# Modulation and first seven projections by slices of 256 features, and the second norm's scale rows moved to the output projection

## The reference

```python
mod = silu(c) @ w_ada + b_ada                      # six vectors of 1024
shift1, scale1, gate1, shift2, scale2, gate2 = split(mod, 6)
h = rms_norm(x, norm1_g) * (1 + scale1) + shift1
q, k, v, qi, ki, wi, u, g_attn, g_pool = split_cols(h @ w_in, IN_SIZES)
# index scores relu(qi ki) wi choose 128 keys for each query; attention; pooling over u
merged = sigmoid(g_attn) * y_attn + sigmoid(g_pool) * y_pool
x = x + gate1 * (merged @ w_out)
h2 = rms_norm(x, norm2_g) * (1 + scale2) + shift2
x = x + gate2 * conv_ffn(h2)
```

## Time and profile before

| | us |
|---|---|
| Median of 3 runs | 754.72 |
| Lowest and highest | 754.32, 757.94 |
| The profiled execution | 759.15 |
| Its span | 757.2 |
| TensorE busy in it | 739.7 (98%) |
| VectorE, ScalarE, GpSimd busy | 379.0, 306.6, 312.3 |

### The profile page before, as it was taken

One profiled execution on the slowest core, in us unless ns is written; L12 is line 12 of the kernel. 1 busy time (PEld: TensorE's weight loads), 2 busy tenths in 40 slices (PEclk: granted clock), 3 DMA queues, 4 the chain that ended last, 5 costly groups with the idle time before them and its releaser, 6 DMA issues.

```text
span 757.2 us, 9497 instructions
## 1 busy us (share of the span) xinstructions
PE 739.7 (98%) x3568; PEld 597.2 (79%) x3568; DVE 379.0 (50%) x693; ACT 306.6 (40%) x501; POOL 312.3 (41%) x165
## 2 busy tenths in 40 slices
PE   4989999999999999999999999999999999999997
PEld 3467788888777777887899888888788888888886
DVE  2588699972446551774685435464443433004002
ACT  4224513256756763334455343434334343212120
POOL 1125338562623332547423444444444444443431
PEclk9969989999999999999999999999999999999999
DMA  8995511221113113644338344323323321233301
GB/s 327 381 338 204 187 55 57 71 97 56 57 57 112 57 56 107 262 159 128 97 95 267 112 111 112 91 76 112 101 68 110 111 99 68 84 112 112 137 2 56
DMA packets 83995, 92.75 MB, mean 122 GB/s; under 512 B 2035, under 2 KB 66287, under 8 KB 83951
## 3 DMA queue, kind: packets, MB, share of 16 engines
q1 hardware_dynamic: 82719, 87.43, 35.6%
q10 hardware_dynamic: 1232, 4.72, 1.7%
HBM read 90.05 MB, written 2.10 MB: 122 GB/s over the span
## 4 chain that ended last, share of the span: by engine, by line
PE 96%; DVE 1%; DMA 1%; ACT 1%; SPq 0%; issue 0%; DVEq 0%; ACTq 0%
PE bank L1471 42%; PE bank L1491 21%; PE bank L1480 21%; PE bank L1547 2%; PE bank L1741 1%; PE bank L1719 1%; PE bank L1707 1%; PE bank L1513 1%; PE bank L1625 1%; DMA xtok<-in_x_dram 1%; PE bank L1565 1%; PE bank L1614 1%; ACT junk L747 1%; PE bank L1518 1%; PE bank L1775 1%; PE bank L1532 0%
## 5 line engine op out<-in xcount | busy, mean ns | idle before, releaser
L650 POOL TENSOR_TENSOR wsplit<-stage,wsplit 128x1024 fp32r<-128x1024 f32 (+1 forms) x120 | 275.0, 2295 | 395.2 <-ACT wsplit L732 391.7
L1471 PE MATMUL bank<-hT,wsplit 128*128 128x512 f32 (+1 forms) x1264 | 295.3, 386 | 0.0
L1471 PEld LDWEIGHTS bank<-hT,wsplit 128*128 128x128 f32 x1264 | 231.8, 190 | 46.5 <-issue 0.9
L732 ACT ACTIVATE wsplit<-stage 128x1024 fp32r<-128x1024 f32 (+1 forms) x120 | 119.8, 1000 | 280.9 <-PE bank L1480 196.7
L1480 PE MATMUL bank<-hT,wsplit 128*128 128x512 f32 (+1 forms) x632 | 152.8, 384 | 0.0
L1480 PEld LDWEIGHTS bank<-hT,wsplit 128*128 128x128 f32 x632 | 114.7, 188 | 23.5 <-issue 0.8
L1491 PE MATMUL bank<-wsplit,guT 128*128 128x512 f32 x528 | 119.8, 389 | 0.0
L1491 PEld LDWEIGHTS bank<-wsplit,guT 128*128 128x128 f32 x528 | 99.1, 188 | 20.5
L1429 DVE SCALAR_TENSOR_TENSOR yb<-bank,conv,yb 128x511 f32<-128x511 f32 (+1 forms) x44 | 32.9, 749 | 65.1 <-ACT yb L1022 64.3
L1429 DVE SCALAR_TENSOR_TENSOR ya<-bank,conv,ya 128x511 f32<-128x511 f32 (+1 forms) x44 | 33.0, 749 | 59.2 <-ACT ya L1022 58.4
L1364 DVE TENSOR_TENSOR tmp_last<-bank,gate_row 128x512 f32<-128x512 f32 x8 | 5.5, 688 | 101.7 <-PE bank L1491 101.7
(11 more groups left out here) (188 smaller groups left out, 731.8 us busy)
## 6 DMA issues: line engine op xcount, KB each, us to landing
stage<-in_w_up_dram SPq DMA_DIRECT2D x44, 512.0 KB, 5.2
stage<-in_w_in_dram SPq DMA_DIRECT2D x17, 1024.0 KB, 5.3
stage<-in_w_down_dram SPq DMA_DIRECT2D x10, 1024.0 KB, 5.0
ada_early<-in_w_ada_dram SPq DMA_DIRECT2D x8, 1024.0 KB, 10.1
ada<-in_w_ada_dram SPq DMA_DIRECT2D x7, 1024.0 KB, 11.7
ada_mid<-in_w_ada_dram ACTq DMA_DIRECT2D x4, 1024.0 KB, 8.1
stage<-in_w_out_dram SPq DMA_DIRECT2D x4, 1024.0 KB, 6.1
ada_last<-in_w_ada_dram SPq DMA_DIRECT2D x4, 1024.0 KB, 11.1
```

The costliest lines, as they stand in the source:

```text
L650: pool.tensor_tensor(unit_split(n, 1), unit_source(n), unit_split(n, 0).bitcast(F32), ALU.subtract).then_inc(low, 1)
L732: me.did(act.activation(unit_split(n, 0), unit_source(n), ACT.Copy), high)
L1471: pe.matmul(out_bank[:, tokens], hi[:, k, :], rhs[:, part, k, tokens], start=k == 0 and part == 0, stop=False)
```

## The change

The start is worked by four slices of 256 features. SP loads for slice q all 1024 rows of the 256 columns of vectors 0 and 1 (2 MB in four transfers of 1 KB pieces) and then one stage item that holds, for two feature blocks, the weights of all seven first units (896 columns). The small vectors are loaded by ScalarE's queue. x is scaled by the inverse root token by token on VectorE before it is turned, into all eight banks. TensorE adds up a slice of the two vectors with a padded c as weights, four groups of 32 output rows in one bank; ScalarE copies the bank, four one-column products add the rows up. VectorE and ScalarE make two blocks of `hT`, and VectorE, no longer GpSimd, makes the low parts of the first eight weight units. TensorE then runs the seven units together for each block.

The index dots, sums and relus stand within v0 and v1; v comes before u. The rows of vector 3 (shift2) are added up during the first products, from eight loads of 512 KB; those of vector 4 (scale2) go by `ada_mid` and stand on VectorE ahead of `gate_vector(0)`, its column sums on TensorE behind the first tile of the second half.

```diff
-ROW_TURN = {1: 0, 3: 1, 4: 2, 2: 3, 5: 4}
+ROW_TURN = {3: 0, 2: 1, 4: 2, 5: 3}
+FIRST = (("qi", 0), ("qi", 1), ("kw", 0), ("q", 0), ("q", 1), ("q", 2), ("q", 3))
+KS = 896
+KQ = KD // 2
...
+            def load_first(q):
+                for half in range(2):
+                    ks = slice(half * KQ, (half + 1) * KQ)
+                    for j in range(2):
+                        c0 = j * D + 2 * q * P
+                        sp.dma_start(ada_first[q][:, ks, 2 * j * P:2 * (j + 1) * P], ada[:, ks, c0:c0 + 2 * P]
+                                     ).then_inc(ada_in[q][half], 16)
...
+            def load_row(k):
+                if k % 4 == 0:
+                    sp.wait_ge(sums_ok, k // 4 + 1)
+                sp.dma_start(ada_row[k][:, :], ada[:, k, 3 * D:4 * D]).then_inc(ada_row_in[k], 16)
             for n, item in enumerate(sch.items):
-                if n == NSTAGE:
-                    for q in range(KD // 2):
-                        load_early(3, q)
+                if n < KQ:
+                    load_first(n)
...
                 load_item(n)
+                if n == KQ - 1:
+                    for k in range(KD):
+                        load_row(k)
...
# ScalarE
             for t in range(NT):
+                act.wait_ge(x_in[t], 16)
                 me.did(act.activation(junk[:, t % 2, :], xtok[:, t, :], ACT.Square,
                                       accum_out=tstat[:, 0, t:t + 1]), x_sum)
+                me.settle()
+                me.did(act.activation(tstat[:, 2, t:t + 1], tstat[:, 0, t:t + 1], ACT.Sqrt, bias=eps[:, 0:1],
+                                      scale=1.0 / D), root_ok)
+            act.wait_ge(x_t, NT)
+            for k in range(0, KD, 2):
+                me.did(act.activation(xT[:, k, :], banks[k][:, :], ACT.Copy), x_kept[0])
+            for q in range(KQ):
+                act.wait_ge(sums_ok, q + 1)
+                me.did(act.activation(rowsum[:, :], OB[:, :], ACT.Copy), row_ok)
+                high_parts(2 * q + 1)
+                for k in (2 * q, 2 * q + 1):
+                    act.wait_ge(n_ok, k + 1)
+                    me.did(act.activation(hT[:, 0, k, :], full1[:, k % 2, :], ACT.Copy), h_hi)
+                high_parts(2 * q + 2)
...
             def load_mid(n):
...
+                j, q = (2, 4)[n // 4], n % 4
+                act.dma_start(ada_mid[n % 2][:, :, :], ada[:, 2 * q:2 * q + 2, j * D:(j + 1) * D]
                               ).then_inc(ada_mid_in[n % 2], 16)
...
+            load_mid(4)
+            load_mid(5)
             high_parts(sch.unit["out", 1, NT - 1] + 1)
+            load_mid(6)
+            load_mid(7)
# VectorE
+            for q in range(KQ):
+                first_vectors(q)
+                for k in (2 * q, 2 * q + 1):
...
+                    me.did(dve.tensor_scalar(full1[:, k % 2, :], xT[:, k, :], gs[:, 0, k:k + 1], mod[:, k:k + 1],
+                                             ALU.mult, ALU.add), n_ok)
+                for k in (2 * q, 2 * q + 1):
+                    first_low(k)
+                    low_parts(k + 1)
+                for k in ((), (0, 1, 2), (3, 4, 5, 6), (7,))[q]:
+                    mod_row_of(3, k)
...
             merged_low(KD - 1)
+            for q in range(KD // 2):
+                mod_rows(4, q)
             gate_vector(0)
# TensorE
+            def first_sums(q):
+                if q == 0:
+                    pe.wait_ge(c_pad, 1)
+                    pe.wait_ge(x_kept[1], 1)
+                else:
+                    pe.wait_ge(first_mod, q)
+                for half in range(2):
+                    pe.wait_ge(ada_in[q][half], 32)
+                    for g in range(KQ):
+                        k = half * KQ + g
+                        mm = pe.matmul(OB[32 * g:32 * (g + 1), :], cpad[:, k, :], ada_first[q][:, k, :],
+                                       start=half == 0, stop=half == 1)
+                mm.then_inc(sums_ok, 1)
...
+            first_sums(0)
+            first_columns(0)
...
+            for k in range(KD - 1):
+                first_products(k, h_hi, 0, 0, start=k == 0)
+                if k % 2:
+                    first_columns(k // 2 + 1)
+                first_products(k, h_lo, 1, 0)
+                first_products(k, h_hi, 0, 1).then_inc(used, 1)
+                if k % 2 == 0 and k < KD - 2:
+                    first_sums(k // 2 + 1)
+            for name in FIRST:
+                first_products(KD - 1, h_hi, 0, 0, (name,))
+                first_products(KD - 1, h_lo, 1, 0, (name,))
+                first_products(KD - 1, h_hi, 0, 1, (name,), stop=True).then_inc(used if name == FIRST[-1] else first_ok, 1)
...
+            index_dots(0)
+            await_bank(pe, ("v", 0))
+            value_high(0, 0, 3)
+            index_dots(2)
+            value_high(0, 3, 6)
+            index_dots(4)
+            value_high(0, 6, 8)
+            value_low(0, 0, 2)
+            index_dots(6)
+            squares(0)
+            value_low(0, 2, 5)
+            index_dots(8)
...
+                if t == 0:
+                    pe.wait_ge(gate_ok, 2)
+                    mod_columns(4)
                 if t == 1:
                     x2_turn(0)
```

More of the change, by code:

```diff
@@ L138, in split, with first @@
             self.unit[name] = len(self.units) - 1
+    def first(self):
+        for q in range(KQ):
+            self.items.append(("first", "in", (C_Q, C_QI), 2 * q, 2 * q + 2, 1))
+            self.last_use.append(None)
+            for r in range(2):
+                self.units.append((1, r, KS))
+                self.house()
+                self.item_of.append(q)
+                self.last_use[q] = ("unit", len(self.units))
+        for at, name in enumerate(FIRST):
+            self.opens(name, "dve", FIRST_BANK[at])
+        self.ring = NBANK - 1
     def block_rows(self, w, k0, k1, half, home=None):
@@ L179, in schedule @@
     s = Schedule()
[L180 removed]
+    s.first()
+    for kind, n in (("v", KA), ("u", KA)):
         for m in range(n):
@@ L1464, in _, with high_products @@
         def _(pe):
-            def high_products(n, out_bank, rhs, tokens=slice(0, S)):
+            def high_products(n, out_bank, rhs, tokens=slice(0, S), blocks=None):
                 hi = unit_split(n, 0)
                 pe.wait_ge(high, n + 1)
-                for k in range(sch.units[n][0]):
+                for k in blocks or range(sch.units[n][0]):
                     for part in range(2):
@@ L1478, in low_products @@
                 pe.wait_ge(low, n + 1)
-                for k in range(nk):
+                for k in blocks or range(nk):
                     mm = pe.matmul(out_bank[:, tokens], lo[:, k, :], rhs[:, 0, k, tokens], start=False,
@@ new lines, in first_columns, with first_products @@
+            def first_columns(q):
+                pe.wait_ge(row_ok, q + 1)
+                for n in range(4):
+                    mm = pe.matmul(OB[:, MC + n:MC + n + 1], rowsum[:, n * P:(n + 1) * P], ones[:, 0:1],
+                                   start=True, stop=True)
+                mm.then_inc(col_ok, 1)
+            def first_products(k, made, part, a, names=FIRST, start=False, stop=False):
+                pe.wait_ge(made, k + 1)
+                pe.wait_ge((high, low)[a], k + 1)
+                for name in names:
+                    at = FIRST_AT[FIRST.index(name)]
+                    mm = pe.matmul(bank(name)[:, :], unit_split(k, a)[:, 0, at:at + P], hT[:, part, k, :],
+                                   start=start, stop=stop)
+                return mm
```

514 lines of the change are left out of this document (234 added, 280 removed).

## The result

| | before | after |
|---|---|---|
| Median, us | 754.92 (6 runs) | 758.38 (6 runs) |
| Lowest and highest | 754.11, 757.94 | 757.46, 760.41 |
| The profiled execution | 759.15 | 758.16 |
| Its span | 757.2 | 756.4 |

The changed kernel takes 1.0044 times as long, with a 95% interval from 1.0024 to 1.0065: 3.5 us slower, just inside 0.5%. The forecast of 754.3 us is 4.1 us too low, and had the sign the other way by a hair. The span that the prediction summed up, 756.8 us, was met within 0.4 us, and the two profiled executions stand the other way round from the medians. So the question for the experiments is less where the gain went than why the profiled execution of before wasn't a typical one.

The account below looks back on a forecast made before the run. TensorE's own work was taken as the bound, 96% of the chain. A start gain of 12.3 us and an output projection loss of 11.9 turned 757.2 into 756.8 us of span; set against the median, 754.3 us, range 745 to 762.

Parts of the forecast that it names:

- The start: From kernel start to the end of product ("k", 0): that point moves from 151.8 to 139.5 us, gain 12.3 us (8 to 16).
- the turned blocks: TensorE's turns of x at the start: 32 blocks at 0.23 us, 7.4 us, starting near 11.7 and ending at 19.1.
- Rival (c): Row sums at the start: column groups don't overlap, 19.6 us more, 773.9; pairs only, 6.4 more, 760.7; chance 0.07.
- One sign of being wrong: At the start: VectorE waiting for an ada row before the third slice would show the forecast wrong.
- rival (d): Start is starved: ada rows land 4 us late, VectorE holds the third slice, 757 to 759 us; chance 0.06.
- The output projection: Second norm's scale rows delay gate_vector(0) to 376.9 and the first normed tile to 388.2: loss 11.9 us (3.7 to 17).
- The second wait: Output projection: TensorE idle again about 3 us before the first turn of xs.
- Rival (a): Output projection hides more of the scale rows: loss 4 to 7 us, 746.4 to 749.5 us; chance 0.32.
- The sum of the span: Whole kernel: 757.2 - 12.3 + 11.9 = 756.8 us of span, 758.8 with the 1.95 around it.
- slow clock: TensorE between q0 and ("k", 0): 3.0 us of u1 and some 0.4 more at low clock, counted as gone.
- the offset: Whole kernel: the profiled execution of before lies 4.43 us above its median, so the forecast becomes 754.72 - 0.4 = 754.3 us.
- Rival (b): Output projection: landings at 8.1 to 10.5, 5 us more, up to 2 of clock, load 7 after 376: 758 to 761; chance 0.17.

## Why the prediction was right and wrong

**The start: right, a little low.** First product 25.9 foretold, 25.36 measured; a slice's row sums 2.0 and 1.92; half rate 5 us at the first products, 5.2 measured; seven units ended 77.0 and 75.1; ("k", 0) 139.5 and 137.85. The gain against the profiled execution was foretold as 12.3 and came out as 151.55 - 137.68 = 13.9 us. Two terms cancelled: the turned blocks cost 5.25 / 32 = 0.16 us and not 0.23, and started 1.9 us later than assumed. Rival (c) is excluded by the run with one group. One sign of being wrong did show, VectorE waiting for rows of vector 3 ahead of the third slice (2.6 and 0.5 us), but TensorE was busy without a gap from 26 to 75 us, so rival (d) fell. Selection cost nothing; VectorE still waited 5.0 us at TensorE's last squares, against 6.66 in the earlier trace rows.

**The output projection: the mechanism right, its sizes partly by luck.** With the start's 13.87 us added, the gate vector ends at 363.57 + 13.87 = 377.4 (foretold 376.9) and the turn of x2 (0) stands at 388.7 (388.2): a loss of 12.3 there against 11.9. To the end of the span the loss is 13.1 (13.9 - 0.8). TensorE's wait was 6.56 us (6.1). Loads 4 and 5 came as foretold, but load 7 took 7.5 us to land and not 5.5; since it was issued 1.3 us sooner than foretold (366.1 against 367.4), it landed only 0.7 us late, at 373.6. The rows beside GpSimd, in the sum with 3.7 us, took 3.3; they slowed GpSimd as well, 11.88 us against the 9.43 of the earlier trace rows. The second wait, 3 us ahead of the turn, didn't come: the low clock stretched the tile over it. The terms that the prediction names between the gate vector and the turn, 5.5 + 3.4 + 1.7, give 387.5 and not the 388.2 that it writes; the 11.3 us that lie between its two times are what was measured. Rival (a) fell: nothing more was hidden.

**The sum of the span: 756.8 foretold, 756.4 measured.** That it fits within 0.4 us is luck in part: the gain was 1.6 us larger than foretold and the loss 1.2 us.

**The step that failed is the next sentence**, "The profiled execution is 4.43 us above the median, so 754.72 - 0.4 = 754.3". It takes for granted that the changed kernel's profiled execution would stand as far above its median. But the 4.43 us weren't a cost of being profiled. The second profile of the same kernel was 4.6 us shorter in span and lay at 754.39, below the median; the 4.6 are the fall at 100 us (3.2) and the longer low clock at the start (1.4). The prediction itself removed both: it counted 3.0 + 0.4 us of "slow clock" as gain and built the start anew in absolute times. So they were taken off twice, once in the gain and once with the offset. The changed kernel's profile, at 758.16, is at its median, 758.38.

Put right with the prediction's own terms, from the execution of before without the fall: 754.4 - (12.3 - 4.6) + 11.9 = 758.6 us, against a measured median of 758.38. The same is said by the 758.8 that stands in the prediction ahead of the offset. Both mean slower by 0.5%, so the sign of the forecast hung on the offset alone. Against an execution of before without the fall the start gains 146.96 - 137.68 = 9.3 us, and the projection loses 13.1.

That the fall is what makes half of before's executions longer rests on these profiles, on the mean clock of 54 executions and on the ten executions with the column sums apart. Why the same instructions are followed by a fall in one execution and not in the next isn't settled. The profiles show only that the fall follows 24 short instructions (in four of the five profiles in which they stand together, that of the moved scale rows among them), and none came there where they stood apart. Rival (b) named the range in which the result lies, 758 to 761, but not its reason. Its landings came in part, 7.5 us for the last load, yet that load landed ahead of the 376 us by which the rival was to be told, and the loss was 1.2 us above the forecast and not 5.

## What to carry to other kernels

If a sum is made against one profiled execution, ask first whether the stalls that the change removes are what sets this execution apart from the median; if so, they must not be taken off again with the offset, and a second profile of the unchanged kernel settles it. A chain of "buffer free, issue, landing" behind operations that take turns with another engine is shortened only in part by making these operations small (3.8 of 13 us here): issue the loads earlier, or let what the critical engine needs go ahead of them. Work moved to a place where its engine idles still delays whatever stands behind it in order; splitting it around the urgent results and issuing its loads earlier won back 9.8 us here.

## What the runs showed of the hardware

- An operation of VectorE with two inputs in SBUF waited for GpSimd's running operation whatever its size: 8 columns took 0.23 us alone and up to 2.32 beside it, 1024 columns 1.28 and 3.3. That is a wait for a turn and no sharing of bandwidth. The Trainium skill, "SBUF — State Buffer", section Who interferes with whom, says that whichever of the two engines issues first holds the port pair that they share for its whole instruction while the other blocks, and that a VectorE instruction with two inputs in SBUF is one that meets GpSimd's reads there; these rows agree.
- Four groups of 32 output rows of TensorE, given instructions in turn, ran 3.7 times as fast as one (1.92 and 7.03 us for 16 instructions).
- One and the same kernel had its TensorE clock fall for 6.7, 3.4, 3.4 and 0 us at the same place, behind eight squares of 2 columns and sixteen one-column products without a wait between them. The longest fall cost 3.2 us of a 755 us kernel. With the two groups apart the spread was 1.6 us, against 3.7 beside it.
